# An encoder trunk on one core: w_out as two more blocks of seven half-size products, and the weight sums moved from VectorE to GpSimd

## The chip, the cores and the metric

The kernel runs on one core of a Trainium2 chip. The metric is the device time of one execution in microseconds, lower is better. Before the change the median of three executions is 1077.69 us (1077.61 to 1077.79). All durations below come from one profiled execution; engines are named as in the profile: PE is TensorE, DVE is VectorE, ACT is ScalarE, POOL is GpSimd, SP is SyncE, which only issues DMAs here.

## The reference

Two layers of this, all in float32, for 256 tokens of width 1024 (h is the normed and modulated input):

```python
proj = h @ w_in[i]
u_hy, q, k, v, gate_hy, gate_at = jnp.split(proj, split_idx, axis=-1)
y_hy = hyena_mixer(u_hy, ...)            # 256 x 768
y_at = dilated_attention_mixer(q, k, v)  # 256 x 256
merged = (jax.nn.sigmoid(gate_hy) * (y_hy @ w_br_h[i])
          + jax.nn.sigmoid(gate_at) * (y_at @ w_br_a[i]))
x = x + g1[:, None, :] * (merged @ w_out[i])
h = modulate(rms_norm(x, norm2_g[i]), sh2, sc2)
x = x + g2[:, None, :] * grouped_moe(h, router_w, router_bias, w1[i], w3[i], w2[i])
```

The change touches three of the matrix products: `y_hy @ w_br_h` (256 x 768 by 768 x 1024), the part `gate_at` of `h @ w_in` and `merged @ w_out` (both 256 x 1024 by 1024 x 1024), and what adds the last one to x.

## The kernel before, in words

Every engine has its program written out by hand, in the order in which it runs; semaphores (`v_sum`, `p_sev` and so on, the first letter is the engine that raises them) tie the programs together, and nothing reorders them. Weights come in blocks of 512 columns through a ring of six 2 MB buffers; SP issues their DMAs in a fixed order, each as soon as the block that lay there before is released (`released`).

A matrix product with all 256 tokens and one block of 512 columns is cut in halves in each of its three directions: two token tiles (`tt`), two halves of the inner dimension, two column halves of 256. Done plainly that is eight products of half size. Four blocks per layer, two of w_br_h (block 0 and 1) and two of the attention gate in w_in (block 2 and 3), are done with seven instead, by the scheme of Strassen and Winograd (`seven`, L1074). It needs four sums over the activations, S1 to S4 (`sum_of`, L1940, shared by the two blocks of a matrix), and four over the weights of each block, M1 to M4 (`mix`, L1951). The seven products, in PE's order, I call P1 to P7:

| product | left | right | goes to bank | then |
|---|---|---|---|---|
| P1 | a11 | b11 | X | ACT keeps it |
| P2 | S1 | M1 | Y | ACT keeps it |
| P3 | S2 | M2 | V | DVE adds it to the first (`first_sums`) |
| P4 | a12 | b21 | X, on top | tile 0, left columns are complete |
| P5 | S3 | b12 (now M3 after the subtraction) | V, new | DVE: tile 1, right columns |
| P6 | S4 | b22 | Y, on top | DVE: tile 0, right columns |
| P7 | a22 | M4 | V, on top | DVE: tile 1, left columns |

(Letters for halves are loose here: the code has signs folded into the sums.) The three PSUM banks X, Y and V are the same for every block, so PE waits before P1, P3, P5 and P7 until DVE has read what lay there. In between (`block_in_seven`) DVE also forms the weight sums of the next block and, in layer 0 only, pieces of the next layer's modulation vectors (`next_part`, one multiply-add of 128x512 each, L1672 to L1676). After the four blocks come two blocks of w_br_a, done plainly (`branch`), and DVE multiplies them with the gates and adds them to `merged` (L2051, L2052). PE transposes merged (L1152), ACT copies it into mT (L1499), and w_out is done plainly: 2 column blocks by 2 token tiles, each 8 matmuls with 512 columns. DVE multiplies each with gate1 and adds it to x (`add_to_x`, L2063, L2064); then x is transposed (`turn_x`), the router's logits are formed (`route`), and the experts begin. Their weights, 96 blocks of 1 MB per layer, fill the rest of the layer.

GpSimd issues DMAs and does nothing else.

## Time and profile before

| | |
|---|---|
| median of three executions | 1077.69 us |
| the profiled execution, its own time | 1078.26 us |
| its span in the trace | 1076.4 us |
| PE busy | 1038.7 us, 97% |
| DVE busy | 527.4 us, 49% |
| ACT busy | 182.1 us, 17% |
| POOL busy | 19.9 us, 2% |
| DMA, mean | 309 GB/s |

The span begins with the first instruction and ends with the last; what the execution's own time has beyond it lies around it. The stretch of the change is 242 to 335 us in layer 0 and 756 to 844 us in layer 1; the experts of the two layers run from about 345 to 553 and from 854 to 1065 us. In the views a 128x256 or 128x512 matmul in float32 counts as two records (x8 for a product of four matmuls), and the time between the starts of two rows is a better measure of what PE spends than the duration of one row, since the duration has the way through the array in it.

### The profile page before, as it was taken

Reading aid. Unit: us, or ns where it says so; the run is one execution under the profiler, and the core shown is the slowest. Engines: PE = TensorE matmul, PEld = TensorE weight load, DVE = VectorE, ACT = ScalarE, POOL = GpSimd, SP = SyncE. Lnnn points to the kernel's source line nnn. Section 1 sums busy time; section 2 is a strip of 40 time slices with the busy share of each in tenths; the row PEclk is TensorE's granted clock in tenths of the full one; section 3 lists DMA queues with packets and bytes.
Section 4 is the critical chain, followed back from the end, with each engine's and each line's share of the span. In section 5 each row is a group of like instructions: output and inputs, shape, how many; then the busy total and the mean of one; then the engine's idle time right before and its main releaser. Section 6 shows DMA issues by size and latency. Waiting matters only on the chain.

```text
span 1076.4 us, 18126 instructions
## 1 busy us (share of the span) xinstructions
PE 1038.7 (97%) x7701; PEld 606.3 (56%) x7701; DVE 527.4 (49%) x1120; ACT 182.1 (17%) x364; POOL 19.9 (2%) x40
## 2 busy tenths in 40 slices
PE   7999999999999999999999999999999999999895
PEld 4688667657846344433448865775774634444231
DVE  3477696668725422351325778764542532222123
ACT  4121100311115113101121110031111410111002
POOL 3000000000000000000000000000000000000000
PEclk9999999999999999999999999999999999999898
DMA  9997845369793999999999975435675399999993
GB/s 309 391 381 260 307 164 185 111 215 331 271 374 133 410 387 422 421 420 421 420 400 392 333 262 197 170 119 195 227 297 219 141 423 420 420 421 420 422 420 139
DMA packets 90920, 332.82 MB, mean 309 GB/s; under 512 B 5020, under 2 KB 5355, under 8 KB 66005
## 3 DMA queue, kind: packets, MB, share of 16 engines
q1 hardware_dynamic: 87905, 323.56, 77.1%
q0 software_dynamic: 2048, 6.09, 1.6%
q10 hardware_dynamic: 884, 1.97, 0.6%
q8 instruction: 63, 1.03, 0.4%
q14 instruction: 20, 0.16, 0.0%
HBM read 330.54 MB, written 1.05 MB: 308 GB/s over the span
## 4 chain that ended last, share of the span: by engine, by line
PE 84%; DVE 7%; DMA 5%; issue 1%; SPq 1%; ACT 1%; DVEq 0%
PE bank L756 81%; DMA ring<-in_moe_w_dram 3%; DMA area<-in_moe_w_dram 2%; SPq L686 1%; PE bank L1028 1%; PE bank L1244 1%; DVE wide L1674 0%; DVE area L1866 0%; DVE wide L1871 0%; DVE area L1869 0%; PE bank L1162 0%; DVE area L1868 0%; DVE area L1867 0%; PE bank L809 0%; DVE wide L1870 0%
## 5 line engine op out<-in xcount | busy, mean ns | idle before, releaser
L756 PE MATMUL bank<-ring,hT 128*32 128x512 f32 (+3 forms) x1808 | 283.4, 551 | 4.9 <-DMA ring<-in_moe_w_dram 2.1
L756 PE MATMUL bank<-hT,ring 128*32 128x256 f32 (+1 forms) x2112 | 214.1, 380 | 0.2 <-DVE hT L1708 0.2
L756 PEld LDWEIGHTS bank<-ring,hT 128*32 128x32 f32 (+2 forms) x1808 | 120.2, 134 | 135.2 <-issue 129.9
L756 PEld LDWEIGHTS bank<-hT,ring 128*32 128x32 f32 (+1 forms) x2112 | 158.2, 132 | 55.8 <-issue 8.7
L756 PE MATMUL bank<-ring,area 128*32 128x512 f32 (+1 forms) x680 | 103.5, 584 | 1.8 <-ACT area L1556 0.9
L756 PE MATMUL bank<-area 32*64 32x64 f32 (+5 forms) x648 | 96.1, 363 | 0.0
L756 PE MATMUL bank<-wide,hT 128*32 128x512 f32 (+1 forms) x376 | 76.8, 584 | 0.0
L2240 DVE TENSOR_TENSOR area<-bank,area 128x512 f32<-128x512 f32 x14 | 9.7, 691 | 130.5 <-PE bank L756 130.5
L756 PEld LDWEIGHTS bank<-area 32*64 32x64 f32 (+4 forms) x648 | 43.7, 145 | 51.7 <-issue 50.4
L1674 DVE SCALAR_TENSOR_TENSOR area<-ring,wide,area 128x512 f32<-128x512 f32 x84 | 63.0, 750 | 2.2
L756 PEld LDWEIGHTS bank<-ring,area 128*32 128x32 f32 (+1 forms) x680 | 31.6, 113 | 52.8 <-issue 49.5
L2251 DVE TENSOR_TENSOR area<-bank,g2b 128x512 f32<-128x512 f32 x28 | 19.4, 691 | 80.4 <-PE bank L756 80.4
L756 PE MATMUL bank<-ring,xn 128*128 128x512 f32 x128 | 55.6, 592 | 0.0
L756 PE MATMUL bank<-ring,wide 128*128 128x256 f32 (+2 forms) x224 | 52.2, 475 | 0.9 <-DVE area L1991 0.9
L756 PE MATMUL bank<-area,xn 128*128 128x128 f32 x448 | 52.5, 275 | 0.1
L756 PEld LDWEIGHTS bank<-area,xn 128*128 128x128 f32 x448 | 51.1, 192 | 0.4 <-issue 0.4
L2170 DVE TENSOR_TENSOR x<-x,bank 128x512 f32<-128x512 f32 x56 | 38.5, 687 | 24.6 <-PE bank L756 24.6
L2156 DVE TENSOR_SCALAR hT<-bank,A,modT 128x128 f32<-128x128 f32 x56 | 19.1, 404 | 52.2 <-PE bank L756 52.2
L756 PEld LDWEIGHTS bank<-ring,xn 128*128 128x128 f32 x128 | 24.0, 190 | 28.7 <-issue 28.7
L756 PEld LDWEIGHTS bank<-ring,wide 128*128 128x128 f32 (+1 forms) x224 | 31.4, 167 | 14.8 <-issue 10.2
L1550 ACT ACTIVATE area<-bank 128x512 f32<-128x512 f32 x14 | 8.4, 597 | 185.2 <-PE bank L756 185.2
L756 PEld LDWEIGHTS bank<-wide,hT 128*32 128x32 f32 (+1 forms) x376 | 24.1, 118 | 27.2 <-issue 26.4
(284 smaller groups left out, 1050.5 us busy)
## 6 DMA issues: line engine op xcount, KB each, us to landing
ring<-in_moe_w_dram SPq DMA_DIRECT2D x136, 1024.0 KB, 15.3
ring<-in_w_in_dram SPq DMA_DIRECT2D x26, 2048.0 KB, 11.4
ring<-in_w_ada_dram SPq DMA_DIRECT2D x24, 2048.0 KB, 14.2
wide<-in_moe_w_dram SPq DMA_DIRECT2D x32, 1024.0 KB, 12.3
cst<-in_moe_w_dram SPq DMA_DIRECT2D x13, 1024.0 KB, 14.6
area<-in_moe_w_dram SPq DMA_DIRECT2D x11, 1024.0 KB, 14.3
ring<-in_w_out_dram SPq DMA_DIRECT2D x4, 2048.0 KB, 7.7
ring<-in_w_br_h_dram SPq DMA_DIRECT2D x4, 1536.0 KB, 7.1
```

The lines of the kernel that those rows point to most:

```text
L686: sp.dma_start(dst.rearrange("p (k f) -> p k f", f=D if m == 2 else FE), t[name][L, experts[e], :, :].rearrange(order, p=P)[:, part, :]).t ...
L756: return pe.matmul(dst, lhsT, rhs, start=start, stop=stop, skip_group_check=True)
L1028: last = pe.transpose(bank[5][:, b * P:(b + 1) * P], prob[:, u, b * P:(b + 1) * P], ident)
L1244: last = pe.transpose(bank[0][:, f * P:(f + 1) * P], act[:, f::NF], ident)
L1550: sc.activation(sil, bank[0][:, :], ACT.Silu).then_inc(a_sil, 1)
L1674: link(dv.scalar_tensor_tensor(part, wk, c, part, ALU.mult, ALU.add))
L2156: last = dv.tensor_scalar(hg[:, k, :], bank[3][:, (k - 4) * P:(k - 3) * P], A2[:, k:k + 1], modT[:, 3 * ND + k:3 * ND + k + 1], ALU.mult, ...
L2170: dv.tensor_tensor(x[:, tt, cols], x[:, tt, cols], bank[2 + 2 * tt + h][:, :], ALU.add)\
L2240: dv.tensor_tensor(act, bank[1][:, :], sil, ALU.mult).then_inc(v_act, 1)
L2251: dv.tensor_tensor(yS[:, cols], bank[6 + h][:, :], g2b[:, cols], ALU.mult).then_inc(v_yS, 1)
```

## The change

1. The two blocks of w_out are also done by `seven`, as blocks 4 and 5 of each layer (`SEVEN = 6`), with their own choice of banks. The sums over merged are formed by DVE once all of mT is there.
2. The partial results of these two blocks are multiplied with gate1 and x is added to them (`with_x`) before the last products come, so that behind P5, P6 and P7 one multiply and one add of 128x256 remain. The sum of squares is collected in quarters.
3. All weight sums, of all six blocks, are issued on GpSimd, 24 instructions a layer. M4 of a block waits until the block before is done, M1 and M2 of the next until P2 and P3 of this one are, since they reuse their room; for block 4 the room is in hT, free after block 3.
4. A ring buffer of a block is released after P7 and not after P6.
5. In PE's program the transposes of x's first tile stand ahead of the last matmul of block 5, and both router products come after those of the second tile.

```diff
-SEVEN = 4
+SEVEN = 6
...
-                return (p_gate, L * 4 + 2 * q + 2) if q < 2 else (p_sev, (L * SEVEN + q) * 7 + 6)
+                return (p_gate, L * 4 + 2 * q + 2) if q < 2 else (p_sev, (L * SEVEN + q) * 7 + 7)
...
             if kind == "out":
-                return p_wo, L * 4 + 2 * b + 2
+                return p_sev, (L * SEVEN + 4 + b) * 7 + 7
...
+                def mix(i, j):
...
+                    if j == 0:
+                        pool.wait_ge(landing, value)
+                    else:
+                        pool.wait_ge(v_mix, n * 4 + j)
+                    if i == 4 and j == 0:
+                        pool.wait_ge(p_sev, n * 7)
+                    elif i and j < 2:
+                        pool.wait_ge(p_sev, (n - 1) * 7 + 2 + j)
+                    if j == 3:
+                        pool.wait_ge(p_sev, n * 7 + (i == 0))
+                    dst, a, b = ((mixed[0], b12, b11), (mixed[1], b22, mixed[0]), (b12, b22, b12),
+                                 (mixed[2], b21, mixed[1]))[j]
+                    pool.tensor_tensor(dst, a, b, ALU.subtract).then_inc(v_mix, 1)
+
+                pool.wait_ge(p_pt, L * UNITS + 4)
+                for j in range(3):
+                    mix(0, j)
+                for i in range(SEVEN):
+                    mix(i, 3)
+                    if i + 1 < SEVEN:
+                        for j in range(3):
+                            mix(i + 1, j)
...
-                    X, Y, V = (bank[b][:, 0:HW] for b in (2, 3, 7))
+                    X, Y, V = (bank[b][:, 0:HW] for b in ((2, 3, 7) if i < 4 else ((3, 1, 2), (0, 3, 1))[i - 4]))
...
+                    if i == 4:
+                        pe.wait_ge(a_mt, L * 4 + 2)
...
-                    product(V, of(1, 1), combined(2), False)
+                    if i < 4:
+                        pe.wait_ge(v_sev, added + 2)
+                    else:
+                        pe.wait_ge(v_wo, L * 8 + (i - 4) * 4 + 2)
+                    product(V, of(1, 1), combined(2), False, turn_x if i == 5 else None)
...
                 for n in range(2):
-                    w = block_of("out", n)
-                    for tt in range(NT):
-                        for k in range(ND):
...
-                            last = mm(bank[2 * n + tt][:, :], mT[:, k, tt * P:(tt + 1) * P], w[:, k, :],
-                                      k == 0, k == ND - 1)
-                        last.then_inc(p_wo, 1)
+                    seven(4 + n, block_of("out", n), mT, sums_m, mixed_m, half_d)
+                keep_clock_short(2, 3)
+                turn_x(1)
                 route(0)
-                keep_clock_short(1, 4)
-                turn_x(1)
-                keep_clock_short(1, 2)
                 route(1)
...
+                def with_x(n):
+
+                    parts = ((both16, 0, 1), (both15, 1, 1), (keep1, 1, 0))
+                    for dst, tt, c in parts:
+                        last = dv.tensor_tensor(dst, dst, gated_cols(n, c), ALU.mult)
+                    link(last)
+                    for dst, tt, c in parts:
+                        last = dv.tensor_tensor(dst, dst, x[:, tt, (2 * n + c) * HW:(2 * n + c + 1) * HW], ALU.add)
+                    link(last)
+
+                def add_to_x(n, j):
+
+                    m, b, tt, c, part = ((4, (3, 0)[n], 0, 0, None), (5, (2, 1)[n], 1, 1, both15),
+                                         (6, (1, 3)[n], 0, 1, both16), (7, (2, 1)[n], 1, 0, keep1))[j]
+                    cols = slice((2 * n + c) * HW, (2 * n + c + 1) * HW)
+                    dv.wait_ge(p_sev, (L * SEVEN + 4 + n) * 7 + m)
+                    link(dv.tensor_tensor(keep5, bank[b][:, 0:HW], gated_cols(n, c), ALU.mult))
+                    dv.tensor_tensor(x[:, tt, cols], part if j else x[:, tt, cols], keep5, ALU.add).then_inc(v_wo, 1)
+                    dv.wait_ge(v_wo, L * 8 + 4 * n + j + 1)
...
+                dv.wait_ge(a_mt, L * 4 + 4)
+                sum_of(4, 0)
+                sum_of(4, 1)
+                sum_of(4, 2)
+                first_sums(4)
+                sum_of(4, 3)
+                with_x(0)
+                add_to_x(0, 0)
                 if L + 1 < DEPTH:
                     shift_and_scale(L + 1)
+                add_to_x(0, 1)
+                add_to_x(0, 2)
+                add_to_x(0, 3)
```

This is DVE's row between P3 of block 2 and the end of that block in layer 0, before the change (L1969 is a weight sum, L1991 adds a finished product, L1672 to L1676 are pieces for the next layer, L1949 is S4):

```order
L1977 TENSOR_TENSOR area<-bank7,area 128x256 [waits p_sev,a_sev]
L1979 TENSOR_TENSOR area<-area 128x256 [waits a_sev]
L1949 TENSOR_TENSOR wide<-hT,wide 128x512 [waits v_sum,v_chain]
L1969 TENSOR_TENSOR area<-ring0 128x1024 [waits p_sev,slot_in0]
L1674 SCALAR_TENSOR_TENSOR area<-ring3,wide,area 128x512
L1991 TENSOR_TENSOR area<-bank7,area 128x256 [waits v_sev,p_sev,v_chain]
L1969 TENSOR_TENSOR area<-ring0,area 128x1024 [waits p_sev,v_mix]
L1674 SCALAR_TENSOR_TENSOR area<-ring3,wide,area 128x512
L1676 SCALAR_TENSOR_TENSOR area<-ring3,wide,area 128x512 [waits v_chain]
L1991 TENSOR_TENSOR area<-bank3,area 128x256 [waits v_sev,p_sev]
L1969 TENSOR_TENSOR ring0<-ring0 128x4x256 [waits v_mix]
```

And the same place now (lines have moved: L2008 is L1977, L2011 is L1979, L2000 is L1949, L1723 and L1725 are L1674 and L1676, L2023 is L1991):

```order
L2008 TENSOR_TENSOR area<-bank7,area 128x256 [waits p_sev,a_sev]
L2011 TENSOR_TENSOR area<-area 128x256 [waits a_sev]
L2000 TENSOR_TENSOR wide<-hT,wide 128x512 [waits v_sum,v_chain]
L1723 SCALAR_TENSOR_TENSOR area<-ring3,wide,area 128x512
L2023 TENSOR_TENSOR area<-bank7,area 128x256 [waits v_sev,p_sev,v_chain]
L1723 SCALAR_TENSOR_TENSOR area<-ring3,wide,area 128x512
L1725 SCALAR_TENSOR_TENSOR area<-ring3,wide,area 128x512 [waits v_chain]
L2023 TENSOR_TENSOR area<-bank3,area 128x256 [waits v_sev,p_sev]
```

The weight sums are gone from between the instructions for which PE waits; the rest keeps its order. On GpSimd, which had no row between its modulation DMAs and those of the next filter, the sums now stand in one line, here those of block 3 and the first of block 4:

```order
L764 TENSOR_TENSOR area<-ring0 128x1024 [waits p_sev,slot_in0]
L764 TENSOR_TENSOR area<-ring0,area 128x1024 [waits p_sev,v_mix]
L764 TENSOR_TENSOR ring0<-ring0 128x4x256 [waits v_mix]
L764 TENSOR_TENSOR wide<-ring0,area 128x1024 [waits p_sev,v_mix]
L764 TENSOR_TENSOR hT<-ring2 128x1024 [waits p_sev,slot_in4]
```

They moved to an engine of their own; each still waits for the one before it (v_mix).

Third, DVE in layer 0 from P3 of the first w_out block to P7's release, where before it had two rows for each 512 columns of one tile:

```order
L2008 TENSOR_TENSOR area<-bank2,area 128x256 [waits p_sev,a_sev]
L2011 TENSOR_TENSOR area<-area 128x256 [waits a_sev]
L2000 TENSOR_TENSOR area<-xn,area 128x512 [waits v_sum,v_chain]
L2084 TENSOR_TENSOR area<-area,wide 128x256 x3
L2087 TENSOR_TENSOR area<-area,x 128x256 [waits v_chain]
L2087 TENSOR_TENSOR area<-area,x 128x256 x2
L2096 TENSOR_TENSOR area<-bank3,wide 128x256 [waits p_sev,v_chain]
L2097 TENSOR_TENSOR x<-x,area 128x256 [waits v_chain]
L1776 TENSOR_TENSOR modT<-bank0,bT 128x16 [waits p_mod,v_wo]
L1777 SCALAR_TENSOR_TENSOR A1<-modT,vT1 128x8 [waits v_chain]
L2096 TENSOR_TENSOR area<-bank2,wide 128x256 [waits p_sev,v_A1]
L2097 TENSOR_TENSOR x<-area 128x256 [waits v_chain]
```

The last two rows read P5 out of bank V and add it to x; P7 goes to the same bank and waits for them. L1776 and L1777 stood ahead of w_out before and stand in this row now.

## Rows read from the trace of the kernel before

**Rows 1.** The page's first lines: span and busy time, instructions.

```profile
span 1076.4 us, 18126 instructions
PE 1038.7 (97%) x7701; PEld 606.3 (56%) x7701; DVE 527.4 (49%) x1120; ACT 182.1 (17%) x364; POOL 19.9 (2%) x40
```

**Rows 2.** Chain of waits that ended last: start us, us, what.

```profile
278.40 20.99 PE bank L756 x88
...
302.08 24.04 PE bank L756 x56
...
528.38 24.43 DMA area<-in_moe_w_dram
...
984.13 28.15 DMA ring<-in_moe_w_dram
```

**Rows 3.** PE's timeline, layer 0: start us, us, operation, xcount, [idle before <-releaser].

```profile
255.44 1.53 PE L756 MATMUL bank<-ring,wide 128*128 128x256 f32 x6 [0.86 <-DVE area L1991]
...
266.00 1.97 PE L756 MATMUL bank<-ring,hT 128*128 128x256 f32 x8 [1.26 <-DVE area L1991]
...
274.71 1.89 PE L756 MATMUL bank<-ring,wide 128*128 128x256 f32 x8
276.44 1.89 PE L756 MATMUL bank<-wide,hT 128*128 128x256 f32 x8
278.40 1.96 PE L756 MATMUL bank<-ring,hT 128*128 128x256 f32 x8
...
300.99 1.09 PE L1152 MATMUL bank<-cst,area 128*128 128x128 f32 x8 [0.73 <-DVE area L2052]
301.92 24.20 PE L756 MATMUL bank<-ring,xn 128*128 128x512 f32 x56
325.96 1.05 PE L1162 MATMUL bank<-cst,x 128*128 128x128 f32 x8
...
330.37 0.64 PE L756 MATMUL bank<-hT,area 128*32 128x128 f32 x16
```

**Rows 4.** PE's timeline, layer 1, start of block 2.

```profile
776.94 1.97 PE L756 MATMUL bank<-ring,hT 128*128 128x256 f32 x8 [0.28 <-DVE area L1991]
```

**Rows 5.** DVE's groups, 242 to 302 us: xcount | busy us, mean ns | idle before.

```profile
L1674 DVE SCALAR_TENSOR_TENSOR area<-ring,wide,area 128x512 f32<-128x512 f32 x12 | 9.0, 746 | 0.1
L1991 DVE TENSOR_TENSOR area<-bank,area 128x256 f32<-128x256 f32 x12 | 5.1, 422 | 2.7 <-PE bank L756 1.9 <-DVE area L1672 0.4 <-DVE area L1674 0.2
...
L1969 DVE TENSOR_TENSOR wide<-ring,wide 128x768 f32<-128x768 f32 x4 | 3.8, 955 | 0.1
...
L2052 DVE TENSOR_TENSOR area<-area 128x512 f32<-128x512 f32 x4 | 2.8, 692 | 0.1
L1983 DVE TENSOR_TENSOR area<-area,xn 128x256 f32<-128x256 f32 x6 | 2.5, 424 | 0.2
L1969 DVE TENSOR_TENSOR area<-ring 128x1024 f32<-128x1024 f32 x2 | 2.4, 1220 | 0.0
```

**Rows 6.** DVE's timeline behind the last w_out product, layer 0.

```profile
330.48 0.69 DVE L2063 TENSOR_TENSOR area<-bank,wide 128x512 f32<-128x512 f32 x1 [3.12 <-PE bank L756]
331.20 0.69 DVE L2064 TENSOR_TENSOR x<-x,area 128x512 f32<-128x512 f32 x1
```

**Rows 7.** ACT's timeline, layer 0: the second half of mT, and xn.

```profile
301.69 1.09 ACT L1499 ACTIVATE xn<-bank 128x512 f32<-128x512 f32 x2 [0.74 <-PE bank L1152]
...
336.03 4.20 ACT L1534 ACTIVATE xn<-x,rs 128x1024 f32<-128x1024 f32 x2
```

**Rows 8.** Busy time by stretch: PE, PEld, DVE, ACT, POOL; PEclk, DMA share, GB/s.

```profile
242.00:302.00 60.00, 57.07 (x271) 46.37 (x270) 46.00 (x75) 9.45 (x22) 0.00 (x0) 1.00 0.83 313
302.00:335.00 33.00, 32.89 (x130) 16.57 (x130) 7.77 (x17) 7.68 (x18) 0.00 (x0) 1.00 0.68 264
```

**Rows 9.** SP's timeline, layer 0: w_out's DMAs, first expert weights.

```profile
263.48 14.88 SPq L691 DMA_DIRECT2D ring<-in_w_out_dram  x2
...
280.02 14.81 SPq L686 DMA_DIRECT2D ring<-in_moe_w_dram  x6
```

More of the change, by code:

```diff
@@ L314, in trunk_kernel @@
             + [chunks(hy[:, 8 * W:10 * W], HW)]
+        sums_m = [chunks(area[:, 2 * D + (1 + b) * W:2 * D + (2 + b) * W], P) for b in range(4)]
+        mixed_m = [chunks(hT[:, 4 * b:4 * b + 4, :].rearrange("p k n -> p (k n)"), HW) for b in range(2)]\
+            + [chunks(hy[:, 12 * W:14 * W], HW)]
         cut[0] = 0
@@ L1072, in _, with turn_x, product @@
                     ada_post(0, L + 1)
+                def turn_x(tt):
+                    pe.wait_ge(v_wo, L * 8 + 7 + tt)
+                    columns = x[:, tt, :].rearrange("p (m k) -> p k m", k=ND)
+                    for k in range(ND):
+                        last = pe.transpose(bank[4 + 2 * tt + k // 4][:, (k % 4) * P:(k % 4 + 1) * P],
+                                            columns[:, k, :], ident)
+                        if k % 4 == 3:
+                            last.then_inc(p_tr, 1)
                 def seven(i, w, src, sums, mixed, kc):
                     n = L * SEVEN + i
-                    X, Y, V = (bank[b][:, 0:HW] for b in (2, 3, 7))
-                    def product(dst, left, right, start):
+                    X, Y, V = (bank[b][:, 0:HW] for b in ((2, 3, 7) if i < 4 else ((3, 1, 2), (0, 3, 1))[i - 4]))
+                    added = first_add(L, i)
+                    sum0 = L * 12 + i // 2 * 4
+                    def product(dst, left, right, start, between=None):
                         for k in range(kc):
+                            if between and k == kc - 1:
+                                between(0)
                             last = mm(dst, left(k), right(k), start and k == 0, k == kc - 1)
@@ L1492, in _ @@
                 last.then_inc(a_yat, 1)
-                for i in range(SEVEN):
+                for i in range(4):
                     keep_products(i)
@@ L1937, in operands @@
                         return x0T, sums_x, mixed_h, half_h, "brh", i
[L1938 removed]
+                    if i < 4:
+                        return hT, sums_h, mixed_d, half_d, "in", IN_A + i
+                    return mT, sums_m, mixed_m, half_d, "out", i - 4
                 def sum_of(i, j):
@@ L1976, in first_sums @@
                     dv.wait_ge(p_sev, n * 7 + 3)
-                    dv.tensor_tensor(both16, bank[7][:, 0:HW], keep1, ALU.add).then_inc(v_sev, 1)
+                    dv.tensor_tensor(both16, bank[(7, 2, 1)[max(0, i - 3)]][:, 0:HW], keep1, ALU.add)\
+                      .then_inc(v_sev, 1)
                     dv.wait_ge(a_sev, n * 2 + 2)
@@ L2038, in _ @@
                 next_sums(1)
-                dv.wait_ge(p_pt, L * UNITS + 4)
-                for j in range(3):
-                    mix(0, j)
                 block_in_seven(0, (2 * ND, 2 * ND + 3))
@@ L2045, in _, with add_to_merged @@
                 block_in_seven(3, (3 * ND + 1, 4 * ND))
-                for q in (2, 3):
+                def add_to_merged(q):
                     for tt in range(NT):
@@ L2058, in _ @@
                                  A2[:, :].unsqueeze(2).to_broadcast([P, ND, NE]), ALU.mult).then_inc(v_ra, 1)
-                def add_to_x(n, tt):
-                    dv.wait_ge(p_wo, L * 4 + 2 * n + tt + 1)
-                    cols = slice(n * W, (n + 1) * W)
-                    link(dv.tensor_tensor(mtmp, bank[2 * n + tt][:, :], g1b[:, cols], ALU.mult))
-                    dv.tensor_tensor(x[:, tt, cols], x[:, tt, cols], mtmp, ALU.add).then_inc(v_wo, 1)
-                    dv.wait_ge(v_wo, L * 4 + 2 * n + tt + 1)
+                first_sums(5)
+                with_x(1)
+                for j in range(3):
+                    add_to_x(1, j)
+                dv.wait_ge(a_chain, L * 4 + 2)
+                dv.scalar_tensor_tensor(sse[:, :], ssq[:, 0, :], EPS, ssq[:, 1, :], ALU.add, ALU.add).then_inc(v_sse, 1)
+                dv.wait_ge(v_sse, 2 * L + 1)
+                dv.tensor_tensor(sse[:, :], sse[:, :], ssq[:, 2, :], ALU.add).then_inc(v_sse, 1)
+                add_to_x(1, 3)
                 def keep_xT(tt):
```

149 lines of the change are left out of this document (65 added, 84 removed).

## The prediction

> **What bounds the kernel now.** I read the page first: PE is busy for 97% of the span, POOL for 2% [rows 1]. Then the chain of waits: in the stretch of the change it runs through PE's matmuls almost without a break, 21.0 us of block 3 and the branch, 24.0 us of w_out; in the experts each layer has one long piece on a DMA, 24.4 us in layer 0 and 28.2 us in layer 1 [rows 2]. Those two pieces start when PE has released buffers, so they move with PE: whatever reaches the experts earlier should end them earlier by as much. So the change is worth what it takes from PE's row between block 0 and the router, less what it makes PE wait. PE's own waits there are for DVE: 0.86 us before block 1, 1.26 before block 2 and 0.73 among the transposes in layer 0 [rows 3], 0.28 before block 2 in layer 1 [rows 4]. The clock is granted in full in the stretch [rows 8], and PE's work can be counted by the spacing of rows.
>
> **Fewer products.** The first 56 records of w_out take 301.92 to 325.96 us, 0.429 us each, and there are 64: 27.5 us a layer [rows 3]. A half-size product, eight records of 256 columns, has a spacing of 276.44 - 274.71 = 1.73 us [rows 3]. Two blocks of seven are 14 x 1.73 = 24.2 us. Gain 3.3 us a layer, 6.6 in all.
>
> **PE's waits for DVE.** DVE loses 16 weight sums a layer, eight of 0.96 us and eight of 1.22 us [rows 5]. They stand between the instructions for which PE waits. Without them the row between P3 of block 0 and the permission for block 1 in layer 0 is two sums, a piece of 0.75, a finished product, two merges, two more pieces and the next finished product [rows 5]: 4.7 us, with the links between them some 5.3 behind P3, against four products of 1.3 us and the small matmuls for the next layer behind them. The 0.86 goes, the 1.26 too (0.1 may stay), the 0.28 and a gap of 0.23 before block 3 (276.44 + 1.73 = 278.17, and the next row is at 278.40 [rows 3]): 2.5 us. The 0.73 stays, since DVE's last merged columns are formed as before.
>
> **The start of w_out.** Before, PE begins as soon as the first quarter of mT is there. Now P1 needs half of it, and P2 needs S1, which needs all: ACT ends at 302.78 [rows 7], the sum of 128x512 takes 0.7 us [rows 5], so 303.6, and P1 lasts from about 302.0 to 303.7. Nothing lost; up to 0.3 a layer if the links between the engines cost more.
>
> **A new wait in block 4.** P7 reuses the bank of P5 and waits for DVE to read it. Behind P3, DVE has: two sums (0.9), S4 (0.7), six instructions of `with_x` (2.1), a multiply and add (0.9), in layer 0 shift_and_scale (0.4), and again a multiply and add (0.9). With 0.3 for the hand-over from PE that is 6.2 us in layer 0 and 5.8 in layer 1, against three products (P4 to P6), 5.2 us. PE waits some 0.7 and 0.4 us: 1.1 lost. Behind it in PE's queue stands all of block 5. In block 5 the same row has no S4 and no shift, and S1 to S4 are there already: no wait.
>
> **The tail.** Behind the last w_out product a multiply and an add of 512 columns stand on the path: 330.37 to 331.89 [rows 3, 6]. Now both are of 256 columns, 0.42 each in place of 0.69 [rows 5]: 0.5 us a layer, 1.0 in all. The order of routing and transposing costs nothing: router product 1 waits for ACT and DVE to copy x's second tile in both versions, and root and square of ACT lie beside the transposes.
>
> **GpSimd.** 24 sums a layer on an engine that is idle for 93 us here [rows 8]. No row shows such an instruction there. Below: DVE's own 1.22 us for 128x1024. Above: ACT passes 128x1024 in 2.1 us [rows 7], and an engine that takes its two inputs one after another at that pace needs 4.2. I take 2.1, the nearer row of another engine, and three quarters of it for w_br_h. What does it bear? Per block four sums follow one another, and a large block lasts 7 x 1.73 = 12.1 us, so up to 2.9 us each they hide behind PE. At 2.1: M4 of a block starts with it and is there 2.2 us later, needed at 10.4; M1 of the next may start behind P2 and is there by 5.7, M2 by 7.9, M3 by 10.1, needed from 13.8 on. For block 4 all four have to fit between the end of block 3 (278.40 + 12.1 = 290.5) and w_out (302.0): 8.8 us, and P2 needs only the first. The first three of block 0 start in the attention part, long before 244 us. At 4.2 the cover is gone: 17.2 against 12.1 us, 5 us late at blocks 2 and 3 each and 3 more at blocks 1 and 5, some 13 us a layer. The modulation DMAs are ahead of the sums in POOL's queue and the next filter's DMAs behind them; they wait for the router anyway, so nobody waits for a sum there.
>
> The Trainium skill has a price for it (GPSIMD Engine Reference, section 3.1): about 2.6 cycles per element for two inputs, 4.5 us measured for 2048 columns. An estimate from that page would be 2.25 us for 1024, which would leave this sum as it is.
>
> **DMAs.** A block's buffer is free one product later, 1.3 to 1.7 us. w_out's two DMAs, issued from 263.48 on, are needed at 290.5 and some 304 us; the first expert weights are issued from 280.02 on, sixty us ahead of their use [rows 9]. Hidden. The buffers of w_out itself come free earlier by what PE gains.
>
> **Sum.** -6.6 - 2.5 - 1.0 + 1.1 = -9.0 us. The profiled execution took 1078.26 us, 0.57 more than the median 1077.69: 1069.3 under the same conditions, 1068.7 as a median.
>
> **Rival B: GpSimd and VectorE shut each other out.** Every sum on POOL reads two tensors from SBUF and writes one there, and so do many of DVE's instructions in the same stretch: the pieces (x12, 746 ns), the merges (x6, 424 ns), the adds to merged (x4, 692 ns) [rows 5], S4 and `with_x`. If the two can't run at the same time, such a DVE instruction stands behind a whole POOL sum of 1.6 or 2.1 us, and DVE is strictly in order, so the finished products for which PE waits stand behind it. Place by place in layer 0: before block 1 the sums M2 and M3 fall among merge and pieces, 3 us; in block 1 and before block 2, two and a half sums of 2.1, 5; in block 2, where S4 and a piece each let one by and some of it is slack, 2; at the branch, where block 4's sums meet the four adds to merged, 5.5; in block 4, S4 and `with_x` behind M2 and M3 of block 5, 4.5: 20 us. In layer 1 without pieces: 0.7, 0, 3.3, 4 and 4.5, 12.5 us. Together 32 over the sum above: 1101 us. It decides from about 1.2 us per sum on: then the waits are what the change gains. For it: POOL works in 75 to 80% of the time from block 1 on, so almost every such DVE instruction meets one. Against it: no row of this trace shows POOL slowing DVE; but no row has POOL reading SBUF beside DVE either, so the trace doesn't exclude it.
>
> The skill states just this (SBUF — State Buffer, section "Who interferes with whom"): a VectorE instruction with two SBUF inputs and a GpSimd instruction that reads SBUF take the shared port pair in turn, and the second blocks fully until the first is done. By that rule the time would be B's. No run here shows it yet.
>
> **Rival C: they share and each is slower.** If DVE's two-input instructions take one and a half times as long beside POOL, the 5.3 us behind P3 of block 0 become 7, and `with_x` and S4 add 1.6 to block 4's wait; over the places above some 12 us: 1080.
>
> **Rival D: the sums take over 3 us each,** for the second input or a cost per instruction: late M2 and M3 from block 2 on. At 4.2 us, 2 x 13 us more: 1095. It decides at 2.9 us.
>
> **Rival E: the products are saved, the waits stay.** A piece of DVE's row that I put beside PE is on the path (links of some 0.1 us between dependent instructions, S1 late), and 5 us of 9 are given back: 1074.
>
> **The numbers.** A measurement tells some 0.2% from no change, 2.2 us. The sum (1065 to 1073) 40%; B (1085 to 1115) 35%; C (1073 to 1088) 13%, spread over all three; D 6%; E 6%, faster. Faster 0.40 + 0.06 and a few from C, 0.48; same 0.07; slower 0.45. The predicted time is that of the likeliest, 1068.7, its own range 1065 to 1073. The range over all cases reaches from 1064 into the middle of B: 1064 to 1104.
>
> **What would show it.** Right: PE's blocks 0 to 3 without idle for DVE; 1.73 us per product in w_out; an idle of 0.4 to 0.8 us before P7 of block 4; POOL's sums 1.9 to 2.5 us from start to start; DVE's pieces still 746 ns and back to back. B would show as DVE rows with a duration or an idle of a whole POOL sum before L1723, L2074 and L2084, and PE idle before block 1, block 2 and P7 of block 4, released by DVE. C: the same rows at 1.0 to 1.2 us. D: PE waits for POOL by v_mix before P2 and P3. The forecast is wrong as a whole if PE reaches the router later than 330 us in layer 0, or if it gets there 4.5 us earlier and the experts don't end earlier.

## The result, and the profile after

The changed kernel takes 1114.4 us (four runs, 1113.2 to 1117.8) against 1077.7 us: ratio 1.0347, 95% interval 1.0334 to 1.0360. It is slower by 36.7 us where the forecast had 9.0 us faster, and it lies 10 us above the end of the range. The profiled execution took 1114.94 us, its span is 1113.1 us.

The page's first lines, in place of [rows 1], and its row of the granted clock in 40 slices:

```profile
span 1113.1 us, 18449 instructions
PE 1043.5 (94%) x7785; PEld 629.6 (57%) x7785; DVE 569.4 (51%) x1146; ACT 187.0 (17%) x388; POOL 130.9 (12%) x88
PEclk9999999998989999999999999999999999999998
```

DVE has lost 32 weight sums, some 35 us of its own work, and gained only the additions of w_out. Yet it is busy for 569 us and not for 527. That is the first thing to ask about. Its groups from 242 to 302 us, in place of [rows 5] (busy us, mean ns | idle before):

```profile
L1723 DVE SCALAR_TENSOR_TENSOR area<-ring,wide,area 128x512 f32<-128x512 f32 x11 | 15.4, 1403 | 0.2
L2015 DVE TENSOR_TENSOR area<-area,xn 128x256 f32<-128x256 f32 x6 | 5.2, 858 | 0.2
L2023 DVE TENSOR_TENSOR area<-bank,area 128x256 f32<-128x256 f32 x12 | 5.1, 422 | 2.1 <-PE bank L792 1.9
L2011 DVE TENSOR_TENSOR area<-area 128x256 f32<-128x256 f32 x4 | 3.0, 756 | 0.0
```

The pieces (L1723) went from 746 to 1403 ns, the merges (L2015) from 424 to 858 ns. The finished products (L2023), which take one input from a bank and one from SBUF, stayed at 422 ns. A mean doesn't say how; two timelines of the same 12 us do. First POOL's, then DVE's (start us, us, operation):

```profile
261.70 2.35 POOL L764 TENSOR_TENSOR area<-ring 128x1024 f32<-128x1024 f32 x1 [5.54 <-PE bank L792]
264.13 2.41 POOL L764 TENSOR_TENSOR area<-ring,area 128x1024 f32<-128x1024 f32 x1
266.62 2.68 POOL L764 TENSOR_TENSOR ring<-ring 128x1024 f32<-128x1024 f32 x1
269.38 2.40 POOL L764 TENSOR_TENSOR wide<-ring,area 128x1024 f32<-128x1024 f32 x1
```

```profile
263.30 1.03 DVE L2011 TENSOR_TENSOR area<-area 128x256 f32<-128x256 f32 x1
264.37 2.72 DVE L1723 SCALAR_TENSOR_TENSOR area<-ring,wide,area 128x512 f32<-128x512 f32 x1
267.13 0.42 DVE L2023 TENSOR_TENSOR area<-bank,area 128x256 f32<-128x256 f32 x1
267.59 2.00 DVE L2015 TENSOR_TENSOR area<-area,xn 128x256 f32<-128x256 f32 x1
269.50 0.41 DVE L2015 TENSOR_TENSOR area<-bank,xn 128x256 f32<-128x256 f32 x1
269.84 2.49 DVE L1723 SCALAR_TENSOR_TENSOR area<-ring,wide,area 128x512 f32<-128x512 f32 x1
```

The piece that DVE starts at 264.37 ends at 267.09: when POOL's sum ends (266.54), plus 0.55 us. The merge of 267.59 ends at 269.59, POOL's sum at 269.30. At 267.13 DVE reads from a bank while POOL runs its sum, and nothing happens to it. Every DVE instruction here that has all its tensors in SBUF and meets a sum stands until that sum is over, and POOL's next sum is late in turn: 2.68 us at 266.62, where the same sum takes 2.42 us at 801.61 in layer 1.

What stands behind that on PE, in place of [rows 3] and [rows 4] (at 309.99 stands the branch, at 334.50 P7 of block 4; the last two rows are the router's product in layer 0 and P7 of block 4 in layer 1):

```profile
257.31 2.90 PE L792 MATMUL bank<-ring,wide 128*128 128x256 f32 x6 [2.83 <-DVE area L2023]
...
272.93 2.87 PE L792 MATMUL bank<-ring,hT 128*128 128x256 f32 x8 [3.70 <-DVE area L2023]
...
309.99 6.07 PE L792 MATMUL bank<-ring,wide 128*128 128x512 f32 x8 [1.52 <-DVE area L2074]
...
334.50 3.00 PE L792 MATMUL bank<-wide,xn 128*128 128x256 f32 x8 [4.63 <-DVE x L2097]
...
353.36 1.18 PE L792 MATMUL bank<-hT,area 128*32 128x128 f32 x32
...
858.85 3.75 PE L792 MATMUL bank<-wide,xn 128*128 128x256 f32 x8 [4.22 <-DVE x L2097]
```

Read two things in each row. In the brackets, the wait: 2.8, 3.7 and 1.5 us, then 4.6 and 4.2 us before P7 of block 4, all for DVE, none for POOL. And in front of it, how long the product behind the wait lasts: 2.90 for six records that took 1.53 before, 3.75 for eight that took 1.97. The wait costs a second time. The same stretches as in [rows 8] show why: the granted clock was 1.00 there (2.4 GHz throughout), and is 0.94 and 0.90 now, a mean over time at 2.4 and at 1.2 GHz:

```profile
242.00:302.00 60.00, 50.70 (x230) 42.53 (x230) 36.23 (x44) 7.61 (x18) 29.86 (x14) 0.94 0.64 238
302.00:335.00 33.00, 24.06 (x91) 15.93 (x91) 25.84 (x31) 4.38 (x11) 17.35 (x7) 0.90 0.74 300
```

The chain of waits, in place of [rows 2]:

```profile
548.67 24.41 DMA area<-in_moe_w_dram
...
580.50 4.09 issue
...
1040.96 27.94 DMA ring<-in_moe_w_dram
```

The router of layer 0 came 20.3 us late (DVE's logits at 355.45, before 335.15; PE's router product at 353.36, past the 330 us that the prediction named as the sign that it is wrong as a whole), and the long piece of the experts on a DMA came 20.3 us late with it (548.67 - 528.38), as long as before. Layer 1 from its start to its logits is 10.4 us longer. Between the two layers 5.9 us more went by: 4.09 us of issue, and the 28 matmuls behind it at a lower clock (7.49 us for 5.79). The sum is 36.6 us, of 36.7 us between the spans.

### The profile page after: what moved, and what is told of

It reads as the page before. It is cut to its first block, busy times and chain, and to the rows that moved or that the text cites. A ratio compares the mean times of both kernels' runs of the same rounds, so it can differ in the third digit from the quotient of the medians.

```text
span 1113.1 us, 18449 instructions
## 1 busy us (share of the span) xinstructions
PE 1043.5 (94%) x7785; PEld 629.6 (57%) x7785; DVE 569.4 (51%) x1146; ACT 187.0 (17%) x388; POOL 130.9 (12%) x88
## 3 DMA queue, kind: packets, MB, share of 16 engines
q10 hardware_dynamic: 884, 1.97, 0.6%
## 4 chain that ended last, share of the span: by engine, by line
PE 78%; DVE 11%; DMA 7%; issue 2%; SPq 1%; ACT 1%; DVEq 0%
PE bank L792 75%; DMA ring<-in_moe_w_dram 3%; DMA ring<-in_w_ada_dram 2%; DMA area<-in_moe_w_dram 2%; DVE area L1723 1%; DVE area L2074 1%; DVE area L2000 1%; SPq L692 1%; PE bank L1064 1%; PE bank L1283 1%; DVE area L2084 1%; DVE area L2011 1%; DVE wide L2000 0%; DVE area L2015 0%; DVE area L2023 0%
## 5 line engine op out<-in xcount | busy, mean ns | idle before, releaser
L792 PE MATMUL bank<-ring,area 128*32 128x512 f32 (+1 forms) x744 | 118.5, 566 | 2.1 <-ACT area L1605 0.9
L792 PEld LDWEIGHTS bank<-ring,area 128*32 128x32 f32 (+1 forms) x744 | 43.7, 120 | 55.4 <-issue 48.9
L1723 DVE SCALAR_TENSOR_TENSOR area<-ring,wide,area 128x512 f32<-128x512 f32 x84 | 71.8, 855 | 2.2
L792 PE MATMUL bank<-ring,wide 128*128 128x256 f32 (+2 forms) x224 | 56.3, 495 | 7.4 <-DVE area L2023 2.8
L2306 DVE TENSOR_TENSOR area<-bank,g2b 128x512 f32<-128x512 f32 x28 | 19.4, 691 | 79.8 <-PE bank L792 79.8
L792 PE MATMUL bank<-cst 128*128 128x256 f32 (+1 forms) x162 | 36.7, 379 | 4.1 <-issue 4.1
L792 PEld LDWEIGHTS bank<-cst 128*128 128x128 f32 x162 | 29.6, 210 | 11.7 <-issue 8.1
## 6 DMA issues: line engine op xcount, KB each, us to landing
wide<-in_moe_w_dram SPq DMA_DIRECT2D x32, 1024.0 KB, 12.2
cst<-in_moe_w_dram SPq DMA_DIRECT2D x13, 1024.0 KB, 14.7
area<-in_moe_w_dram SPq DMA_DIRECT2D x11, 1024.0 KB, 14.3
```

What stands on the lines that cost most here:

```text
L792: return pe.matmul(dst, lhsT, rhs, start=start, stop=stop, skip_group_check=True)
L1723: link(dv.scalar_tensor_tensor(part, wk, c, part, ALU.mult, ALU.add))
L2306: dv.tensor_tensor(yS[:, cols], bank[6 + h][:, :], g2b[:, cols], ALU.mult).then_inc(v_yS, 1)
```

## The experiments

Theory X is rival B: a GpSimd sum and an all-SBUF DVE instruction shut each other out. All ratios are to the kernel before on the same chip in the same session (1077.7, 1078.2 and 1077.8 us in the three sessions).

**All sums back to DVE.** `mix` is DVE's again, w_out keeps seven products.

```diff
+                    mix(i, 3)          # in block_in_seven, and mix(i + 1, 0..2) as before
...
+                mix(4, 0)
                 add_to_merged(2)
+                mix(4, 1)
+                mix(4, 2)
                 add_to_merged(3)
```

> The changed kernel with all 24 weight sums per layer given back to DVE, so that GpSimd does nothing there; w_out keeps its seven products. Blocks 0 to 3 have their sums where the kernel before had them, block 4's M1 stands ahead of the first branch merge, M2 and M3 between the merges, M4 behind S4, block 5's among the additions to x. Theory X (exclusion: a GpSimd sum and a DVE instruction whose operands all lie in SBUF shut each other out, and that is the whole loss): near the forecast of case A, 1068 to 1074 us, no GpSimd work, DVE sums of 0.75 us everywhere, the router's DVE row of layer 0 near 333 us or earlier. Rival S (the seven products of w_out, with their additions ahead and their lone matmuls of 256 columns, cost the time and not GpSimd): stays at 1095 us or more, with PE waits in blocks 4 and 5 as in the changed kernel (4.6 us before P7 of block 4).

Measured: 1084.0 us (nine runs, 1080.8 to 1092.4), ratio 1.0073 (1.0051 to 1.0095). Rival S is out, since 30 of the 36.7 us are gone; but the forecast, 1068 to 1074, was missed by 10 us. DVE's order was poor: PE waits 2.06 us in the branch behind M1 to M3, and here:

```profile
315.83 1.97 PE L762 MATMUL bank<-wide,xn 128*128 128x256 f32 x8 [3.21 <-DVE x L2100]
```

**Only the four blocks' sums on GpSimd.** The kernel before, with blocks 0 to 3 in the changed kernel's manner.

```diff
+                for i in range(SEVEN):       # on pool, SEVEN = 4
+                    mix(i, 3)
...
-                    mix(i, 3)                # on DVE
                     first_sums(i)
```

> The kernel before, w_out by plain products, with only the weight sums of its four blocks of seven moved to GpSimd in the changed kernel's order. Theory X: the waits of PE that the changed kernel has ahead of block 4 come with it: in layer 0 2.8 + 1.0 + 3.7 + 0.4 + 1.3 + 3.2 + 0.7 = 13 us, in layer 1 1.0 + 0.6 + 1.3 + 0.8 + 2.7 = 6.4 us, and some 3 to 6 us of the lower clock behind them, less 2.5 us of DVE waits that go: 1094 to 1101 us. Rival S (w_out's seven products are the loss): 1075 to 1079 us.

Measured: 1092.4 us, ratio 1.0137 (1.0120 to 1.0154): 2 us below the range, and far from rival S. The waits before and in blocks 1 and 2 of layer 0 are the changed kernel's to a hundredth (2.83, 0.97, 3.70, 0.42, 1.31), here the one before block 2:

```profile
272.44 3.75 PE L784 MATMUL bank<-ring,hT 128*128 128x256 f32 x8 [3.70 <-DVE area L1999]
```

**Only w_out's sums on GpSimd.** The other side: blocks 0 to 3 on DVE, 4 and 5 on GpSimd.

```diff
+                for i in (4, 5):             # on pool
+                    for j in range(4):
+                        mix(i, j)
```

> The kernel with w_out in seven products, the weight sums of blocks 0 to 3 on DVE where the kernel before has them, and only those of blocks 4 and 5 on GpSimd (8 of 24 per layer). Theory X (a GpSimd sum and an all-SBUF DVE instruction exclude each other): what the changed kernel lost beyond the run with only the four blocks' sums moved (1114.4 less 1092.4 = 22 us) was lost in the branch and in block 4, where M1 to M3 of block 4 stand beside the merges and the sums of block 5 beside the additions ahead. So the waits of PE there come back (3.2 us in the branch of layer 0, 4.6 and 4.2 us before P7 of block 4), and the time is 1092 to 1100 us, at least 8 us over the 1084 us with all sums on DVE. Rival (the losses need GpSimd busy throughout, and DVE late from blocks 0 to 3 on): 1080 to 1087 us.

Measured: 1097.4 us, ratio 1.0182 (1.0165 to 1.0199). P7 of block 4 waits 4.63 and 4.22 us, as in the changed kernel. The two parts cost 14.7 and 19.2 us over before, 33.9 together, against 36.7 for both at once: within 3 us, the loss is made up place by place.

**The same sums in halves, and in chunks of 256 columns.**

```diff
-                    pool.tensor_tensor(dst, a, b, ALU.subtract).then_inc(v_mix, 1)
+                    pool.tensor_tensor(dst[:, 0:half], a[:, 0:half], b[:, 0:half], ALU.subtract)
+                    pool.tensor_tensor(dst[:, half:kc], a[:, half:kc], b[:, half:kc], ALU.subtract).then_inc(v_mix, 1)
```

> The changed kernel with each GpSimd sum issued as two halves, one behind the other, so that the same work stands in instructions half as long. Theory X (a DVE instruction waits for the end of the GpSimd instruction that runs): the DVE instruction gets in between the halves; DVE's all-SBUF instructions of 0.7 us take 1.3 to 2.1 us instead of 2.7 us, PE's 4.6 us wait before P7 of block 4 falls to 2 to 3 us, and the time to 1093 to 1105 us. Rival C (the two engines share a bandwidth, and each goes slower while both run): the length of an instruction changes nothing, 1112 to 1118 us, and DVE's instructions keep means near 1.48 us.

> The changed kernel with each GpSimd sum in three or four instructions of 256 columns. Theory X: a DVE instruction waits for 0.6 to 0.9 us at most; all-SBUF instructions of DVE fall to a mean of 0.9 to 1.0 us, but GpSimd and DVE still share one way in, taking turns, and the sums take longer in all. 1078 to 1088 us, less than with halves (1091.1), more than with DVE alone (1067.7). Rival: what an instruction costs GpSimd to start makes its sums the bound: 1090 us or more, with PE waits that end on GpSimd.

Measured: 1091.1 us in halves (ratio 1.0133, 1.0116 to 1.0150) and 1086.5 us in chunks (1.0074, 1.0047 to 1.0101). The pieces' means over 242 to 342 us, in halves and in chunks; whole sums made it 1484 ns:

```profile
L1725 DVE SCALAR_TENSOR_TENSOR area<-ring,wide,area 128x512 f32<-128x512 f32 x12 | 13.7, 1139 | 0.2
```

```profile
L1725 DVE SCALAR_TENSOR_TENSOR area<-ring,wide,area 128x512 f32<-128x512 f32 x12 | 10.8, 897 | 0.2
```

GpSimd does the same work in all three, so a shared bandwidth (rival C) can't explain 23 and 28 us. What a single DVE instruction loses goes by the length of the GpSimd instruction that it stands behind: PE's waits before blocks 1 and 2 fell from 2.83 and 3.70 us to 1.43 and 1.55 in halves and to 0.63 and 0.59 in chunks. The time in halves is 2 us below the forecast's range. But one part of that forecast, a wait of 2 to 3 us before P7 of block 4, did not come. First in halves, then in chunks, for 4.63 us with whole sums:

```profile
322.12 3.75 PE L794 MATMUL bank<-wide,xn 128*128 128x256 f32 x8 [5.44 <-DVE x L2099]
```

```profile
315.82 3.75 PE L794 MATMUL bank<-wide,xn 128*128 128x256 f32 x8 [4.60 <-DVE x L2099]
```

There S4 and the six short instructions of `with_x` follow one another on DVE, and more of them meet a piece of a sum when the sums are cut: the first three of `with_x` took 3.23 us beside whole sums, 4.30 in halves, 2.68 in chunks, where the last three then took 2.56 us for 1.09. So cutting the sums helps a long DVE instruction that stands alone, not a chain of short ones.

**GpSimd only writes.** A memset in place of each sum; the weight sums are left out.

```diff
-                    pool.tensor_tensor(dst, a, b, ALU.subtract).then_inc(v_mix, 1)
+                    pool.memset(dst, 0.0).then_inc(v_mix, 1)
```

> The changed kernel with each GpSimd sum replaced by a memset of the same output, at the same place and behind the same waits: GpSimd reads nothing there (the weight sums are left out). Theory X in the form that only GpSimd instructions which read two SBUF operands shut DVE out: DVE's all-SBUF instructions go back to 0.75 us, the waits go, 1068 to 1076 us. Theory X in the form that any SBUF access of GpSimd does: a memset of 128x768 takes perhaps 0.8 to 1.6 us, DVE's waits are as long as what is left of it, 1080 to 1095 us. Rival D (the chain of signals between PE, GpSimd and DVE sets the time and not the durations): stays within 5 us of 1114 us.

Measured: 1070.0 us (1069.7 to 1071.4), ratio 0.9928 (0.9912 to 0.9945). First POOL's and DVE's groups, 242 to 342 us, then P7 of block 4 on PE:

```profile
L764 POOL MEMSET ring<- 128x1024 f32 x4 | 3.8, 953 | 0.2
...
L1723 DVE SCALAR_TENSOR_TENSOR area<-ring,wide,area 128x512 f32<-128x512 f32 x12 | 9.0, 747 | 0.2
```

```profile
310.10 1.97 PE L792 MATMUL bank<-wide,xn 128*128 128x256 f32 x8 [0.94 <-DVE x L2097]
```

The signals, the program and its order are the changed kernel's, and the forecast's time is there: so the chain of signals, which the expectation calls rival D, costs nothing, and neither do GpSimd's writes. (The prediction's rival D is another one, sums of over 3 us.) The time can be compared although the sums are left out, since the experts did as much as before: the program ran 18,447 instructions, the changed kernel 18,449.

**GpSimd copies.** One SBUF input; the sums are left out again.

```diff
-                    pool.tensor_tensor(dst, a, b, ALU.subtract).then_inc(v_mix, 1)
+                    pool.tensor_copy(dst, a).then_inc(v_mix, 1)
```

> The changed kernel with each GpSimd sum replaced by a copy of its first operand into the same output, behind the same waits: one SBUF input where the sum has two (the sums themselves are left out). Theory X in the form that only GpSimd instructions with two SBUF inputs shut DVE out (the memset, which has none, did not): DVE's all-SBUF instructions stay at 0.75 us and the time is 1069 to 1073 us as with the memset. In the form that any GpSimd instruction that reads SBUF does: DVE waits for what is left of a copy, perhaps 1 to 1.5 us: 1080 to 1095 us.

Its 3482 us say nothing: without the sums other numbers reach the router, and the program ran 26,774 instructions in place of 18,449. Only layer 0 up to the router can be read. POOL's rows, then DVE's of the same time:

```profile
258.51 1.04 POOL L764 COPY area<-ring 128x1024 f32<-128x1024 f32 x1 [0.25 <-PE bank L792]
259.61 1.11 POOL L764 COPY ring<-ring 128x1024 f32<-128x1024 f32 x1
```

```profile
258.82 1.00 DVE L2011 TENSOR_TENSOR area<-area 128x256 f32<-128x256 f32 x1
259.86 1.41 DVE L1723 SCALAR_TENSOR_TENSOR area<-ring,wide,area 128x512 f32<-128x512 f32 x1
```

Reading one tensor is enough to shut DVE out (0.42 became 1.00, 0.75 became 1.41), but the copy is over sooner: PE waits 2.23 us before P7 of block 4, between the memset's 0.94 and the sums' 4.63. The Trainium skill draws the line in the same place (SBUF — State Buffer, "Who interferes with whom"): a VectorE instruction with two SBUF inputs stands against GpSimd instructions that read SBUF, and not against those that only write it. These runs agree: a piece took 1.41 us beside the copy and 0.75 us beside the memset.

**Waits filled.** To tell the waits from the clock behind them, PE multiplies by the identity, into a free bank, while it waits.

```diff
+                    if L == 0 and i in (1, 2):
+                        fill_clock((6, 8)[i - 1])      # 20, 27 in the first version
                     if 0 < i < 4:
                         pe.wait_ge(v_sev, added - 1)
...
+                    if i == 4:
+                        fill_clock(9)                  # 30 in the first version
```

> The changed kernel with PE kept at work while it waits: matmuls on the identity into a free bank, 20 and 27 before blocks 1 and 2 of layer 0, 12 and 10 around block 5's neighbour in the branch of layer 0, 30 before P7 of block 4 in both layers, each group a little shorter than its wait. The waits stay; what goes is the lower clock behind them. Theory K (the products behind a long wait run at the lower clock, and this is lost beside the wait): 2.90, 2.87, 6.07, 3.00 and 3.75 us for the products behind the waits become 1.53, 1.97, 3.68, 1.97 and 1.97 us, the time 1104 to 1110 us. Rival: the lower clock is made up by shorter waits behind it, or the filling itself delays what it precedes: 1112 to 1117 us.

> The kernel with filled waits again, with the filling in its right size: one such matmul took 0.44 us there, so 6 and 8 before blocks 1 and 2 of layer 0 (2.7 and 3.6 us for waits of 2.8 and 3.7), 3 and 3 in the branch (1.3 us for 1.65 and 1.5), 9 before P7 of block 4 (4.0 us for 4.6 and 4.2). Theory K: the products behind the waits run at the full clock, the waits end where they did, and the time falls by the 7 to 9 us that those products took too long: 1104 to 1109 us. Rival: the lower clock costs nothing at the end, since what is late is DVE: 1112 to 1116 us.

Groups of 3 and 3 stand in the branch as well (12 and 10 in the first version). The first was a blunder of size: a matmul on fp32 of 256 columns leaves two records and takes 0.44 us, not 0.11. The filling outlasted the waits, and the time was 1136.0 us. In the right size it is 1100.8 us (1100.0 to 1101.9), ratio 1.0214 (1.0198 to 1.0229), 13.6 us below the changed kernel's 1114.4 and 3 us below the forecast's range. Its PE before block 1 and in block 4:

```profile
254.59 2.84 PE L792 MATMUL bank<-cst 128*128 128x256 f32 x12
257.48 1.56 PE L792 MATMUL bank<-ring,wide 128*128 128x256 f32 x6
...
325.46 4.05 PE L792 MATMUL bank<-cst 128*128 128x256 f32 x18
330.17 1.99 PE L792 MATMUL bank<-wide,xn 128*128 128x256 f32 x8 [0.65 <-DVE x L2107]
```

```profile
302.00:335.00 33.00, 29.75 (x134) 22.79 (x133) 25.87 (x31) 4.49 (x13) 16.86 (x7) 1.00 0.70 278
```

Block 1 starts no earlier (257.48 against 257.31), but its first product lasts 1.56 us and not 2.90, and the granted clock is 1.00. So the loss falls into two parts that can be told apart by the starts of PE's rows. These are the lengths of the stretches, in us:

| PE, from .. to | memset | waits filled | changed | changed again |
|---|---|---|---|---|
| layer 0: block 0 .. block 1 | 10.08 | 13.18 | 13.25 | 13.27 |
| block 1 .. block 2 | 9.30 | 14.16 | 15.62 | 15.77 |
| block 2 .. block 3 | 12.16 | 14.42 | 16.07 | 17.26 |
| block 3 .. transposes of merged | 20.74 | 25.58 | 26.90 | 27.04 |
| transposes .. P7 of block 4 | 14.24 | 18.53 | 18.60 | 18.62 |
| P7 .. router's product | 17.17 | 17.19 | 18.86 | 19.31 |
| layer 1: block 0 .. router's product | 80.43 | 91.34 | 94.10 | 95.81 |

The second column less the first is what the waits cost: 19.4 us in layer 0 and 10.9 in layer 1, 30.3 us. The third less the second is what the products behind them lost at the lower clock: 6.2 and 2.8 us, 9.0 in all. The spans of these two executions differ by 14.3 us; the rest of that, 5.5 us, lies between the two layers, where the filling does nothing: the idle time of issue in the chain of waits above, with the 28 slow matmuls behind it. The last column is the next run.

**The changed kernel again.**

> The changed kernel once more, unchanged, for one question: PE stood still for 4.1 us of issue between the layers of its first profile, and the 28 matmuls behind it that hold the clock took 7.5 us and not 5.8; with the all-DVE versions and with the halves this idle time is 0, with the memset 1.6 us. If it belongs to this program (place of its instructions, or the time at which it comes there), it is 4 us again and the run near 1114 us; if it is chance, it is anything from 0 to 4 us, and the run 1108 to 1116 us.

1113.6 us (one execution), 12.8 us over the filled version in the same session, and no idle between the layers this time:

```profile
583.08 5.79 PE L792 MATMUL bank<-cst 128*128 128x256 f32 x28
```

In its place layer 0 took 2.4 us more, layer 1 1.7 us more, each with more of its products at the lower clock (0.91 and 0.88 in the two stretches above, for 0.94 and 0.90): 8.2 and 4.5 us over the filled version, 12.7 in all. So the lower clock cost 9.0 us in one execution and 12.7 in the other, by the same waits; one of 2.66 us among the transposes of layer 1 was followed by the lower clock here (1.97 us for eight records) and not before (1.09 us). And the 5.9 us between the layers are no part of the mechanism. The idle of issue there comes and goes: 4.1 us, 0, 1.6 with the memset, 3.5 in chunks, 0 in the others (the copying run aside). Why PE issued nothing there stays open.

**Before, with one weight sum moved.** The last question was what the seven products of w_out are worth when DVE's order is right. First the order alone:

```diff
                     quarter(i, 0)
-                    if i < 3:
-                        mix(i + 1, 1)
                     fill(2)
                     quarter(i, 1)
                     if i < 3:
+                        mix(i + 1, 1)
                         mix(i + 1, 2)
```

> The kernel before, w_out by plain products, with one thing moved on DVE: in blocks 0 to 2 the second weight sum of the next block stands behind the second quarter and not ahead of the two part sums. If the waits of PE before blocks 1 and 2 (0.86 and 1.26 us in layer 0, 0.28 in layer 1) come from DVE's order alone, they go and the time falls by 2.1 to 2.4 us, to 1075.3 us; the rest of what the best version gained (10.6 us) is then w_out's. Rival: P3 of the next block waits for the sum instead, no change, 1077.7 us.

Measured: 1075.4 us (nine runs, 1074.5 to 1075.7), ratio 0.9975 (0.9965 to 0.9985). The three waits are gone. That is what moving 16 sums a layer off DVE was to bring (2.5 us), for nothing.

**All sums on DVE, placed.** With that order, M1 to M3 of block 4 in block 3, and DVE's row in block 4 cleared:

```diff
-        sums_m = [chunks(area[:, 2 * D + (1 + b) * W:2 * D + (2 + b) * W], P) for b in range(4)]
+        sums_m = [chunks(hT[:, 2 * b:2 * b + 2, :].rearrange("p k n -> p (k n)"), P) for b in range(4)]
...
+        mixed_m = mixed_d[0:2]\
...
+                    if i == 3:
+                        mix(4, 0)
                     first_sums(i)
...
+                mix(4, 3)
                 dv.wait_ge(a_mt, L * 4 + 4)
-                sum_of(4, 0)
-                sum_of(4, 1)
-                sum_of(4, 2)
+                for j in range(4):
+                    sum_of(4, j)
+                mix(5, 0)
                 first_sums(4)
-                sum_of(4, 3)
                 with_x(0)
                 add_to_x(0, 0)
                 add_to_x(0, 1)
+                mix(5, 1)
```

> All weight sums on DVE, w_out in seven products, and DVE's order changed: M1 to M3 of block 4 stand in block 3, their results in the two buffers that block 3 has read by then (the input sums of w_out go to the buffer of the last inputs), M4 and all four S before the first additions, M1 of block 5 ahead of them and the rest behind the second addition to x; in blocks 0 to 2 the second weight sum for the next block stands behind the second quarter. If only the place of the work on DVE made the 3.2 and 2.1 us waits of the first version with all sums on DVE, they go to 0.0 to 0.5 and 0.7 us, those before blocks 1 and 2 (0.9 and 1.3 us) go as well, and with 6.6 us fewer of products the time is 1067 to 1072 us, under the kernel before. Rival (DVE has no room for 8 more sums: 566 us busy against 527): the waits only move, 1076 to 1084 us.

Measured: 1067.7 us (four runs, 1067.1 to 1069.6), ratio 0.9907 (0.9891 to 0.9924), the fastest of all: 10.6 us under the kernel before, 47 under the changed one. Of these, the order alone brings 2.4 (the run above); the other 8 are the seven products of w_out and the shorter tail, for which the prediction counts 6.6 + 1.0. Its page, P7 of block 4, and the two stretches:

```profile
PE 1028.4 (96%) x7785; PEld 622.6 (58%) x7785; DVE 566.9 (53%) x1194; ACT 186.6 (18%) x388; POOL 20.3 (2%) x40
```

```profile
298.17 1.09 PE L1182 MATMUL bank<-cst,area 128*128 128x128 f32 x8 [0.74 <-DVE area L2080]
...
309.55 1.97 PE L762 MATMUL bank<-wide,xn 128*128 128x256 f32 x8
...
326.72 1.18 PE L762 MATMUL bank<-hT,area 128*32 128x128 f32 x32
```

```profile
242.00:302.00 60.00, 59.13 (x283) 48.68 (x283) 51.26 (x77) 10.38 (x24) 0.00 (x0) 1.00 0.89 339
302.00:335.00 33.00, 32.48 (x194) 27.88 (x192) 26.21 (x73) 14.23 (x30) 2.17 (x4) 1.00 0.74 283
```

DVE is as busy as in the changed kernel (567 us against 569), but with work and not with standing. There was room for the sums on DVE all along: 51 of 60 us in the stretch where the sums were taken away to relieve it.

## Why the prediction was wrong

The step that failed is the one under GpSimd and the waits for DVE: DVE's row was added up with durations from a trace in which POOL was idle (0.75 a piece, 0.42 a merge), as if they held beside 24 sums a layer. The runs showed in their place pieces of 1.40 us and merges of 0.86 us on average, and 30 us of waits for DVE. Rival B said that they might not hold, where and by how much, and it was set at 35% against 40%: the argument against it was only that no row showed it, and no row could have. That the stated range reaches into B, up to 1104, is no merit of the sum: the forecast was faster, and the time went the other way.

- **Fewer products, DVE's waits gone, tail, new wait: -9.0 us.** Right in mechanism and size. The memset run, which has just these terms, is 7.7 us below before. From block 0 to DVE's logits it takes 4.9 us less in layer 0 and 3.6 less in layer 1, 8.5 in all; its idle between the layers takes part of this back. The wait before P7 of block 4, put at 0.7 and 0.4 us, was 0.94 and 0.53. That was a slip in the sum: its own terms, 6.2 and 5.8 us on DVE against 5.2 on PE, give 1.0 and 0.6, and with them the sum is -8.5 us.
- **GpSimd's price.** Put at 2.1 us for 128x1024 and three quarters for 128x768. Measured 2.35 and 1.80 us when free, up to 2.88 and 2.32 in collision. That is at most just under the 2.9 us at which rival D decides, and no PE wait ended on POOL. The estimate from the Trainium skill (GPSIMD Engine Reference, section 3.1), 2.25 us, was nearer.
- **Rival B's places, layer 0:** 3, 5, 2, 5.5 and 4.5 us; measured, filled version less memset version in the table above, 3.1, 4.9, 2.3, 4.8 and 4.3. Layer 1: 0.7, 0, 3.3, 4 and 4.5; measured 10.9 for 12.5 us, of it nothing in blocks 0 and 1. Together 32 us over the sum were forecast for it, and the filled version (1100.8) stands 30.8 us above the memset version (1070.0): with the clock held, B's 1101 us came true, and not by errors that cancel. Only its share of POOL was too high: 75 to 80% were said, and POOL was busy for 50% of 242 to 302 us and 53% of 302 to 335 us.
- **What B lacked: the clock, 9 to 13 us.** All sums of the prediction count PE's work at the full clock, for the rows showed it so [rows 8]. They showed it for a PE that waited 1.26 us at most in that stretch. The changed kernel's 1114.4 us are 13.6 over 1100.8. In its first profile the lower clock took 9.0 us and 5.5 were lost between the layers; in its second the lower clock took 12.7.
- **Rival C** fell with the halves, **D** (sums of over 3 us) with the durations on POOL. **DMAs:** as said; the experts' pieces moved with PE, 20.3 for 20.3 us.

So 36.7 = -7.7 + 30.8 + 13.6. The last two are differences of medians from different sessions; how much of each is the idle between the layers is known only for the profiled executions.

## What to carry to other kernels

Before work goes to GpSimd, list the VectorE instructions beside it that have all their tensors in SBUF: each stands behind what is left of a GpSimd instruction that reads SBUF, and those behind it in order too, while VectorE itself does the same sum in half the time (1.22 us for 2.35 here). Durations from a trace hold only beside the work that ran beside them there. A wait of some us on PE is to be priced with the products behind it at the lower clock: here 9 to 13 us on top of 30. And an engine at 50% busy has room: look for a better place in its own row first, which here brought 10 us where the offload cost 37. Cutting the offloaded work into shorter instructions gave back 23 to 28 of these 37 us, but nothing at the place where short VectorE instructions follow one another.

## What the runs showed of the hardware

- A DVE instruction shut out lasts until the GpSimd instruction's end and then somewhat less than its own time: 0.55 us for a piece of 0.75, 0.3 for a merge of 0.42. With one input from a bank it is not held (0.42 us). A DVE tensor_scalar with one SBUF input is held too: L1721 took 1.92 us in the changed kernel at 249.64, and 0.48 us at 288.75, when POOL ran no sum beside it, or with all sums on DVE.
- GpSimd free: sum of 128x1024 2.35 us, copy 1.04, memset 0.95; of 128x768 1.80, 0.83 and 0.74. A sum of 128x768 in three chunks took 2.09 us, so an instruction more costs it some 0.15 us.
- Behind 2.23 us of waiting (the copying run) the eight records of P7 took 2.99 us in place of 1.97; a wait of 2.66 us was followed by slower records in one execution of the changed kernel and not in the other.
- The same program differs in where it loses: 20.3 or 22.7 us in layer 0, 5.9 or 0.3 us between the layers, 10.4 or 12.2 us in layer 1, and the sum was the same within 1.4 us.
